# Both norms of layer 0: table loads placed ahead, ten taps of the last chunk on TensorE, sums ahead of squares, four first projections of layer 1 grown together

## What is computed

```python
# layer 0
a, gl, z = split(x @ w_in, 3)
u = a * sigmoid(gl)
c = causal_depthwise_conv(concat(state, u), dw_w)           # width 31
y = silu(layer_norm(c + dw_b, ln_g, ln_b)) * silu(z)        # the first norm
x = layer_norm(ALPHA * x + y @ w_out, norm_g[0], norm_b[0]) # the second norm
# layer 1
h = x @ attn_w_in        # per group q, k, v; and z
x = layer_norm(ALPHA * x + attention(h) @ attn_w_out, norm_g[1], norm_b[1])
```

## Time and profile before

| | |
|---|---|
| median of three runs | 1289.85 us |
| the profiled execution, its span | 1294.41 us, 1292.6 us |
| PE / weight load / DVE / ACT / POOL busy | 90% / 79% / 43% / 33% / 17% |
| mean granted clock of TensorE | 0.954 |
| bytes moved by DMA | 372.98 MB, mean 289 GB/s |
| chain that ended last, by engine | PE 74%, DVE 9%, DMA 7%, issue 4%, SP's queue 3%, ACT 3% |

### The profile page before, as it was taken

One profiled execution on the slowest core, in us unless ns is written; L12 is line 12 of the kernel. 1 busy time (PEld: TensorE's weight loads), 2 busy tenths in 40 slices (PEclk: granted clock), 3 DMA queues, 4 the chain that ended last, 5 costly groups with the idle time before them and its releaser, 6 DMA issues.

```text
span 1292.6 us, 27816 instructions
## 1 busy us (share of the span) xinstructions
PE 1158.1 (90%) x11392; PEld 1021.8 (79%) x11392; DVE 559.0 (43%) x1530; ACT 420.3 (33%) x860; POOL 216.7 (17%) x98
## 2 busy tenths in 40 slices
PE   7799999398599998999998899999699999958996
PEld 6688887297598997898887789888599888846656
DVE  3999999878603106034114323400423411254324
ACT  4564455533524224123214113321313311321122
POOL 0000000000222222222222122122122222212100
PEclk9899999699799999999999899999899999979997
DMA  8965579999999799579769578877956977986662
GB/s 298 359 237 215 204 256 304 322 363 352 325 375 384 281 378 349 206 251 362 279 237 382 199 254 317 320 280 278 352 187 223 379 261 275 341 318 254 252 245 90
DMA packets 67683, 372.98 MB, mean 289 GB/s; under 512 B 11632, under 2 KB 14576, under 8 KB 64880
## 3 DMA queue, kind: packets, MB, share of 16 engines
q1 hardware_dynamic: 67568, 371.27, 80.1%
HBM read 353.61 MB, written 192.21 MB: 422 GB/s over the span
## 4 chain that ended last, share of the span: by engine, by line
PE 74%; DVE 9%; DMA 7%; issue 4%; SPq 3%; ACT 3%; POOL 0%; DVEq 0%; ACTq 0%; POOLq 0%
PE pairB L507 11%; PE pairA L507 10%; PE pairB L508 8%; PE pairA L508 8%; DMA ring<-k_tiles 6%; PE pairC L705 3%; PE pairA L517 3%; PE pairB L517 2%; PE pairA L518 2%; PE pairC L549 2%; PE pairA L890 2%; PE pairB L518 2%; PE pairD L658 2%; PE pairB L890 2%; PE pairC L658 1%
## 5 line engine op out<-in xcount | busy, mean ns | idle before, releaser
L1223 POOL TENSOR_TENSOR w_lo<-landing,w_hi 128x1024 fp32r<-128x1024 f32 x86 | 205.0, 2384 | 641.4 <-ACT w_hi L968 641.4
L968 ACT ACTIVATE w_hi<-landing 128x1024 fp32r<-128x1024 f32 x86 | 90.9, 1057 | 437.4 <-PE pairB L508 223.4
L507 PE MATMUL pairA<-act_hi,w_hi 128*128 128x320 f32 x312 | 102.3, 328 | 21.9 <-issue 18.9
L1576 DVE COPY v_nat<-pairA 128x512 f32<-128x512 f32 x12 | 8.3, 692 | 248.5 <-PE pairA L778 248.5
L507 PE MATMUL pairB<-act_hi,w_hi 128*128 128x320 f32 x312 | 100.6, 322 | 0.0
L507 PE MATMUL pairA<-act_lo,w_hi 128*128 128x320 f32 x312 | 98.5, 316 | 0.0
L507 PE MATMUL pairA<-act_hi,w_lo 128*128 128x320 f32 x312 | 98.3, 315 | 0.0
L507 PE MATMUL pairB<-act_hi,w_lo 128*128 128x320 f32 x312 | 97.3, 312 | 0.0
L507 PE MATMUL pairB<-act_lo,w_hi 128*128 128x320 f32 x312 | 97.3, 312 | 0.0
L508 PE MATMUL pairA<-act_lo,w_hi 128*128 128x256 f32 x312 | 88.7, 284 | 0.0
L508 PE MATMUL pairA<-act_hi,w_hi 128*128 128x256 f32 x312 | 88.7, 284 | 0.0
(11 more groups left out here) (394 smaller groups left out, 2851.1 us busy)
## 6 DMA issues: line engine op xcount, KB each, us to landing
kept<-cache SPq DMA_DIRECT2D x64, 2040.0 KB
landing<-w_units SPq DMA_DIRECT2D x120, 512.0 KB, 7.2
ring<-k_tiles SPq DMA_DIRECT2D x104, 512.0 KB, 6.1
ring<-v_tiles SPq DMA_DIRECT2D x104, 512.0 KB, 5.6
kept<-cache SPq DMA_DIRECT2D x16, 2016.0 KB
kept<-cache SPq DMA_DIRECT2D x8, 960.0 KB
kv_new<-kT SPq DMA_DIRECT2D x24, 288.0 KB, 3.3
kv_new<-vT SPq DMA_DIRECT2D x24, 288.0 KB, 5.2
```

The costliest lines, as they stand in the source:

```text
L507: pe.matmul(tok(s, 0, SPLIT), lhs, x[:, k, 0:SPLIT], start=first, stop=last)
L968: act.activation(w_hi[:, m % 2, :], landing[:, m % LAND, :], ACT.Copy).then_inc(hi_done, 1)
L1223: return pool.tensor_tensor(dst, src, hi.bitcast(F32), ALU.subtract)
```

## The change

In the convolution, the last chunk has ten taps on PE (two sets of five diagonals, in both halves of the diagonal buffer) and 21 on DVE. A dummy activation of one column (`load_table`) is put where the tables for Sqrt and Silu are to be loaded. The last square of the first norm goes ahead of the last two silus of z. In the gate loop the low half of a chunk is written behind its own gate, ahead of the next centring. In the second norm the totals of sums stand ahead of those of squares, the running sum of squares has one chunk less (the last two go to PE singly), one centring stands ahead of the variance and one ahead of the reciprocal, and the low half of a chunk follows one chunk behind its scale. ACT and DVE split units 34 and 35 there, to layer 0's slots; units 32 to 35 then grow together in pairs A to D, the last two chunks unit by unit. In `group(0, True)` PE skips the first four units and waits for the evacuation of unit 35 before the first turn of v; ACT splits units 36 and 37 ahead of the evacuations of 32 and 33; POOL clears q_row and p_col only when unit 35 is done, and splits from unit 36 on. SP's program is not changed.

```diff
+LAST_PE_TAPS = 2 * PE_TAPS
+LAST_DVE_TAPS = W - LAST_PE_TAPS
...
# PE
             def conv_taps(j):
                 pe.wait_ge(u_done, 2 * j + 2)
-                pe.wait_ge(diag_done, (j + 1) * PE_TAPS)
+                n = PE_TAPS if j < KC - 1 else LAST_PE_TAPS
+                pe.wait_ge(diag_done, j * PE_TAPS + n)
...
-                for w in range(PE_TAPS):
-                    mm = pe.matmul(C[:, 512:512 + SEQ], diag[:, j % 2, w, :], u_in[:, j, w:w + SEQ],
-                                   start=w == 0, stop=w == PE_TAPS - 1)
+                for w in range(n):
+                    mm = pe.matmul(C[:, 512:512 + SEQ], diag[:, (j + w // PE_TAPS) % 2, w % PE_TAPS, :], u_in[:, j, w:w + SEQ],
+                                   start=w == 0, stop=w == n - 1)
...
+            def out_sum_of(x, of, first, last):
+                pe.matmul(tok(x, 0, SPLIT), ones[:, :], of[:, 0:SPLIT], start=first, stop=last)
+                return pe.matmul(tok(x, SPLIT, NT), ones[:, :], of[:, SPLIT:NT], start=first, stop=last)
...
             pe.wait_ge(sum_added, KC - 2)
-            pe.wait_ge(sq_added, KC - 2)
-            out_sums(sg[:, 0, :], sg[:, 1, :], True, False)
+            out_sum_of(2, sg[:, 0, :], True, False)
+            pe.wait_ge(sq_added, KC - 3)
+            out_sum_of(3, sg[:, 1, :], True, False)
             pe.wait_ge(out_cent, KC)
-            out_sums(res[:, KC - 1, :], sq[:, (KC - 1) % 2, :], False, True).then_inc(out_sqsum, 1)
-            for m in range(2):
+            out_sum_of(2, res[:, KC - 1, :], False, True).then_inc(out_sum, 1)
+            for k in (KC - 2, KC - 1):
+                pe.wait_ge(out_sq, k + 1)
+                mm = out_sum_of(3, sq[:, k % 2, :], False, k == KC - 1)
+            mm.then_inc(out_sqsum, 1)
+            for m in range(4):
                 pe.wait_ge(w_split, LAND + N_IN1 + m + 1)
             pe.wait_ge(out_part, KC)
-            for k in range(KC):
-                pe.wait_ge(y_split, k + 1)
-                for m in range(2):
-                    for q in range(3):
-                        mm = product(m, N_IN1 + m, k, q, act_hi, act_lo, m)
-                    if k == KC - 1:
+            pe.wait_ge(out_var, 2)
+            for ks in (*((k,) for k in range(KC - 2)), (KC - 2, KC - 1)):
+                pe.wait_ge(y_split, ks[-1] + 1)
+                for m in range(4):
+                    for k in ks:
+                        for q in range(3):
+                            mm = product(m, N_IN1 + m, k, q, act_hi, act_lo)
+                    if ks[-1] == KC - 1:
                         mm.then_inc(proj_done, 1)
...
-                        if not (first and m < 2):
+                        if not (first and m < 4):
                             unit(N_IN1 + hg * U_HG + m, m % 2, act_hi, act_lo)
...
+                            elif first and i == 3:
+                                pe.wait_ge(qkv_out, 4)
...
# ACT
+            def load_table(func):
+                act.activation(warm[:, :], vec[:, 0, V_EPS:V_EPS + 1], func)
             for k in range(KC):
+                if k == KC - 2:
+                    conv_square(KC - 1)
                 act.activation(zs[:, k, :], zs[:, k, :], ACT.Silu).then_inc(silu_done, 1)
-            conv_square(KC - 1)
...
+            load_table(ACT.Sqrt)
             act.wait_ge(conv_sqsum, KC)
...
             act.activation(std[:, :], std[:, :], ACT.Sqrt, bias=vec[:, 0, V_EPS:V_EPS + 1]).then_inc(conv_std, 1)
+            load_table(ACT.Silu)
...
-            for m in range(4, KC):
-                out_square(m)
+            out_square(4)
+            out_square(5)
+            hi0(N_IN1 + 2)
+            out_square(6)
+            out_square(7)
+            hi0(N_IN1 + 3)
+            load_table(ACT.Sqrt)
             act.wait_ge(out_sum, 1)
...
-                        if i < U_CH - 2:
+                        if first and m < 2:
+                            hi0(N_IN1 + m + 4)
+                        elif i < U_CH - 2 and not (first and m < 4):
                             split_hi(N_IN1, hg, U_HG, m + 2)
...
# POOL
-            pool.wait_ge(w_split, LAND + N_IN1 + 2)
+            pool.wait_ge(proj_done, N_IN1 + 4)
             pool.memset(q_row[:, :, :, :, :, :], 0.0).then_inc(rows_cleared, 1)
             pool.memset(p_col[:, :, :], 0.0).then_inc(rows_cleared, 1)
...
+            for m in range(4, U_HG + 2):
+                split_lo(N_IN1, 0, 0, m)
+            with pool.Fori(1, HG) as hg:
+                for m in range(2, U_HG + 2):
+                    split_lo(N_IN1, hg, U_HG, m)
# DVE
             for k in range(KC):
                 gate(k)
                 if k + 2 < KC:
                     conv_scale(k + 2)
+                gate_low(k)
                 if k + 3 < KC:
                     conv_center(k + 3)
-                if k:
-                    gate_low(k - 1)
-            gate_low(KC - 1)
...
-            add_square(6)
+            lo0(N_IN1 + 2)
+            lo0(N_IN1 + 3)
             dve.wait_ge(out_mean, 1)
             dve.tensor_tensor(rstd[:, :], neg_mean[:, :], neg_mean[:, :], ALU.mult).then_inc(out_var, 1)
+            take_mean(0)
...
-            for k in range(3):
-                take_mean(k)
+            take_mean(1)
             dve.wait_ge(out_std, 1)
             dve.reciprocal(rstd[:, :], std[:, :]).then_inc(out_rstd, 1)
...
+            out_scale(0)
+            for k in range(KC):
+                if k + 2 < KC:
+                    take_mean(k + 2)
+                if k + 1 < KC:
+                    out_scale(k + 1)
+                dve.wait_ge(y_hi, k + 1)
+                dve.wait_ge(y_ready, k + 1)
+                lo(act_lo[:, k, :], res[:, k, :], act_hi[:, k, :]).then_inc(y_split, 1)
```

More of the change, by code:

```diff
@@ L136, in build @@
         head_mask = sb("head_mask_sb", [P, 2 * P])
+        warm = sb("warm", [P, 1])
         pick = sb("pick_sb", [P, 4 * NQ])
@@ L323, in o_own, with evac_pair @@
             return s_probs[:, bh, 0:2 * P]
+        def evac_pair(first, m):
+            return m if first and m < 4 else m % 2
         def turned_bank(b, h):
@@ L509, in unit, with product @@
                 mm.then_inc(proj_done, 1)
-            def product(out, p, k, q, hi, lo_, s=None):
-                w = (hi_of(p), hi_of(p), lo_of(p))[q] if s is None else (w_hi, w_hi, w_lo)[q][:, s, :]
+            def product(out, p, k, q, hi, lo_):
+                w = (hi_of(p), hi_of(p), lo_of(p))[q]
                 x = (hi, lo_, hi)[q]
@@ L812, in group @@
                         m = ch * U_CH + i
-                        if i >= 2:
+                        if first and m in (4, 5):
+                            pe.wait_ge(qkv_out, m - 3)
+                        elif i >= 2 and not (first and m < 4):
                             pe.wait_ge(qkv_out, hg * U_HG + m - 1)
@@ L990, in diagonals @@
                     act.wait_ge(pe_added, j - 1)
-                for w in range(PE_TAPS):
-                    act.activation(diag[:, j % 2, w, :], ident[:, :], ACT.Copy, scale=vec[:, j, w:w + 1])\
-                        .then_inc(diag_done, 1)
+                for w in range(PE_TAPS if j < KC - 1 else LAST_PE_TAPS):
+                    if w == PE_TAPS:
+                        act.wait_ge(pe_added, j)
+                    act.activation(diag[:, (j + w // PE_TAPS) % 2, w % PE_TAPS, :], ident[:, :], ACT.Copy,
+                                   scale=vec[:, j, w:w + 1]).then_inc(diag_done, 1)
             def sample_products(j, lo_, hi_):
@@ L1145, in group @@
                         if kept is not None:
-                            act.activation(kept, tok(m % 2, 0, NS), ACT.Silu if kind == "z" else ACT.Copy)
+                            act.activation(kept, tok(evac_pair(first, m), 0, NS), ACT.Silu if kind == "z" else ACT.Copy)
                         if kind == "z":
@@ L1238, in _ @@
             pool.wait_ge(y_ready, KC)
-            pool.wait_ge(w_split, LAND + N_IN1 + 2)
+            pool.wait_ge(proj_done, N_IN1 + 4)
             pool.memset(q_row[:, :, :, :, :, :], 0.0).then_inc(rows_cleared, 1)
             pool.memset(p_col[:, :, :], 0.0).then_inc(rows_cleared, 1)
-            with pool.Fori(0, HG) as hg:
-                for ch in range(2):
-                    for i in range(U_CH):
-                        split_lo(N_IN1, hg, U_HG, ch * U_CH + i + 2)
+            for m in range(4, U_HG + 2):
[3 more added lines that the diff above has]
+                    split_lo(N_IN1, hg, U_HG, m)
             for k in range(0, KC, 2):
@@ L1285, in taps @@
                 for i in range(lo_, hi_):
-                    w, q = PE_TAPS + i, j * DVE_TAPS + i
+                    w, q = (PE_TAPS if j < KC - 1 else LAST_PE_TAPS) + i, j * DVE_TAPS + i
                     x, acc = u_in[:, j, w:w + SEQ], odd_sum[:, j % 2, :] if i % 2 else res[:, j, NS:NT]
@@ L1316, in merge @@
                 acc = res[:, j, NS:NT]
-                dve.wait_ge(conv, (j + 1) * DVE_TAPS)
```

(3 more changed lines are left out.)

32 lines of the change are left out of this document (12 added, 20 removed).

## The result

The changed kernel took 1295.65 us (median of 20 runs, 1287.5 to 1302.38), the kernel before 1290.11 beside it: ratio 1.003, 95% interval 1.0016 to 1.0044, or 3.9 us slower (2.1 to 5.7). The profiled execution took 1294.65 us (span 1292.6, the same as before).

A forecast was written before the change was run, and what follows sets the result against it. PE was taken as the bound, with full DMA engines and unit 36's landing 4.5 us behind; the front's 10.7 us vanish there, and +0.26 and +1.4 give +1.7: 1291.6 us on the median, range 1284 to 1297.

The forecast's parts named there:

- The mechanism: Around unit 36: its landing stays at 359.98, ACT's split precedes four evacuations, and PE idles 11 us before turning v.
- Conv norm and gate: Layer 0's first norm and gate: norm -0.9 us, gate -2.95, so the output projection moves by -3.85.
- The ten taps: Convolution's last chunk: about 4.4 us more matmuls on PE; the taps DVE is spared buy nothing.
- Out norm: Layer 0's second norm: reciprocal at 320.85, -4.5 us, with the landing of unit 35 at 314.53 as limit.
- The sum: Start of unit 36 on PE: 369.7 against 368.04, +1.7 us, bounds +0.3 and +4.1.
- the clock: PE's turn of v after idling, starting at 1.2 GHz: costs 1.4 us, between nothing and 3.85.
- The median: Whole kernel: the forecast difference put on the three-run median of 1289.85, giving 1291.6 us.
- rival B: Copies ahead of unit 36 take longer and the change pays the late landing in full: +6.2 to +8.7 us; chance 0.15.
- Rival A: Unit 36 lands sooner than 360 and starts on PE at 362.1: -5.9 to -8.3 us, middle -7; chance 0.13.
- The table load on the path: Silu table load before z's evacuation: 1.28 us without drain; a drain of about 1.38 would make the total +3.1.

The follow-up runs named there:

- e1: The changed kernel with SP's loads of weight units 36 to 38 issued ahead of the six cache copies; ratio 0.9987 to the kernel before.
- e2: The changed kernel with ACT's high halves of units 36 and 37 behind the evacuations of units 32 to 35; ratio 1.0005 to the kernel before.
- e4: The changed kernel with two more 2040 KB cache copies ahead of the load of unit 36; ratio 1.015 to the kernel before.
- e7: The changed kernel without units 32 to 35 grown together (splits and turn of v as before); ratio 0.9973 to the kernel before.
- e9: The changed kernel itself, measured again on another occasion; ratio 1.005 to the kernel before.
- e10: The changed kernel with five taps of the last chunk on TensorE instead of ten; ratio 1.0015 to the kernel before.
- e5: The changed kernel with loads of units 36 to 38 ahead of six copies and POOL's low halves of 36 and 37 ahead of its memsets; 1280.97 us, ratio 0.9927.
- e6: The changed kernel with loads 36 to 38 ahead of the copies, POOL's low halves ahead of its memsets, and five taps instead of ten; ratio 0.9916.
- e11: The changed kernel without the three table loads ahead; ratio 1.0045 to the kernel before.
- e12: The kernel before with two more 2040 KB cache copies ahead of the load of unit 36; ratio 1.0071 to the kernel before.
- e3: The kernel before with SP's loads of units 36 to 38 issued ahead of the six copies; ratio 1.0195 to the kernel before.

## Why the prediction came out as it did

- *The mechanism* was right in each of its steps: full DMA engines, a landing that does not move (359.0 for the forecast 359.98), ACT's split in front of the four evacuations, the turn of v behind the fourth, PE idle for 10.3 us and then at the lower clock. e1, e2, e4 and e7 each take one of its parts away, or add to it, and the start of unit 36 follows in the traces; the times follow as well, in e2 within the noise.
- *Conv norm and gate*: -3.85 forecast for the first mid_lo, -4.2 measured from the burst. The ten taps buy next to nothing there (0.25 us later in e9 than in e10, 0.9 sooner in e5 than in e6), and the table loads 0.8 (e9 against e11) where the Silu load was put at 1.3 less 0.4.
- *Out norm*: the reciprocal at 320.37 against 320.85 looks better than it is; this execution was 2.2 us early, so the norm is 1.7 us later than forecast. I had the landing of unit 35 in the sum as the limit and missed that of unit 32, for which ACT waits 4.41 us and PE then 1.98. Unit 35 had landed at 313.8 (issued at 287.32, 26.5 to landing) when ACT came to split it at 314.31, straight from the last square, so it was not waited for. From there to the reciprocal it took 6.06 us, where I had 6.32 (the pieces that I listed add up to 6.03, with a centring at 0.75). It cost nothing, as everything ahead of 359.
- *The sum* was +1.7 at unit 36 and is +3.3. Term by term: landing 0 forecast, +1.26 measured (154.06 from the burst against 152.80; it lies between 150.8 and 155.5 in the traces with six copies ahead, so this is the scatter of a landing and not the change, and it arises ahead of unit 35, whose landing is 1.45 later, while from there to unit 36 it took 45.2 us against 45.4); from the landing to the turn of v +0.26 forecast, +0.45 measured (6.06 against 5.61); the clock 1.4 forecast, 1.63 measured (4.08 against 2.45). The bounds for the clock, 0 and 3.85, were far too wide on the upper side, because the first products of unit 36 run at full clock again. On the other hand the bounds of the sum, +0.3 and +4.1, hold the clock alone: the 358 to 362 that I gave the landing, worth 2 us each way, are not in them. That +3.3 lies inside is luck in so far: one term's bound was too wide, and another term had none.
- *The median* moved by 3.9 and 6.5 us on two occasions, where +1.7 was forecast. The first interval, 2.1 to 5.7, does not hold +1.7. Beside the terms above there is half of what rival B describes: with ACT ahead of the evacuations a late landing goes to the end in full, while the kernel before absorbs 4.0 us of it (e12). The 4.5 us read from the trace before was about the right size. B's other half, copies that take longer, shows in no trace: seven copies and a load take 44.7 to 45.7 us in all eight with this order. And the landing of unit 36 was not late as a rule: its mean over the seven such traces of the changed kernel and its variants is 152.8, as before. What the rest of the two medians is stays open.
- *Rival A* did not occur: unit 36 took 64.5 us to land, behind every copy issued ahead of it. Given by order (e1), its place for unit 36 does occur: 362.1 forecast, 362.46 measured. Its gain does not: counted from the burst that is 4.5 us sooner than before, not 5.9, and the time fell by only 1.7 us (the interval leaves 5.3 less to 1.9 more), where A had 7.
- *The table load on the path*: z_new starts at 364.16, 0.01 us behind the end of the load (362.87 + 1.28), and the load 0.02 behind vT. The drain that the Trainium skill gives ("ScalarE: Activation LUTs", What ACT_TABLE_LOAD costs) has no room here either; leaving it out was right. The +3.1 that the sum would have been with it is near the measured +3.3 by accident: the terms above make up the 3.3 without a drain.

## What to carry to other kernels

Before speeding up a stretch, look for the first thing behind it that is not paced by an engine: here a load behind 45 us of bulk copies in the same queue, whose landing takes all that the front gains. When such a wait exists, what stands behind the waiting instruction on its engine decides between gain and loss, so put work that is ready (evacuations) ahead of work that waits for a transfer, and loads that are needed soon ahead of copies that nobody waits for. But never put into that queue an instruction that blocks on a late event ahead of bulk work: idle DMA time comes back as a wait later (e3, 25 us).

## What the runs showed of the hardware

- A wait of 3.25 us of PE (e1) was followed by 3.5 us at a granted clock of 0.54, one of 3.35 us (e2) by 0.63, and one of 2.92 us in the kernel before (at unit 34, which starts at 351.37) by 0.60, while behind waits of 1.4 and 1.5 us (the turn of v in e1, e2 and e5) it stayed at 1.00. In e1 the short wait behind the turn cost 1.5 us more than its own length.
- From the landing of unit 35 to that of unit 36, seven copies of 2040 KB and a load took 44.7 to 45.7 us in the eight traces with this order, and nine copies and a load 58.4 (e12) and 58.5 (e4): 6.2 to 6.3 us a copy each time. What scatters is the landing of unit 35, ahead of these copies: 105.5 to 110.6 us from the burst in the same ten traces.
